# Norm factors by one-column sums, a GpSimd power and identity matmuls, and a forget gate's logarithm by a series, in an eight-core decoder layer

## The reference

```
def rmsnorm(x, g):
    y = xf * lax.rsqrt(jnp.mean(xf * xf, axis=-1, keepdims=True) + EPS)
    return y * g
def layernorm(x, g, b):
    mu = mean(x); var = mean((x - mu) ** 2)
    return (x - mu) * lax.rsqrt(var + EPS) * g + b

h = rmsnorm(x, g_mix_pre)
a_val, a_gate, q, k, v, f_logit = split(h @ w_in)
u = causal_depthwise_conv(a_val * sigmoid(a_gate), conv_w, conv_b)    # width 31
conv_out = silu(layernorm(u, conv_ln_g, conv_ln_b))
log_f = log_sigmoid(f_logit + b_forget)                               # 8 heads
c = cumsum(log_f)                                                     # over tokens
attn = softmax(q k^T / 8 + c[t] - c[s], causal) v                     # 8 heads of 64
x = x + rmsnorm(concat(conv_out, attn) @ w_out, g_mix_post)
h = rmsnorm(x, g_ffn_pre)
x = x + rmsnorm((silu(h @ w_gate) * (h @ w_up)) @ w_down, g_ffn_post) # 2816 wide
```

## Time and profile before

| | |
|---|---|
| median of 3 runs | 2541.02 us (2537.87 to 2663.91) |
| profiled execution, slowest of 8 cores (core 1) | 2540.7 us |
| all cores | 2524.0 to 2540.7 us |
| TensorE busy | 2392.3 us (94%) |
| ScalarE busy | 1604.2 us (63%) |
| VectorE busy | 994.6 us (39%) |
| GpSimd busy | 531.4 us (21%) |
| granted TensorE clock, mean of core 1 | 0.976 |

### The profile page before, as it was taken

How to read it: one execution, slowest core, us unless ns; L and a number is a source line. 1 busy time by engine, 2 the same in 40 slices (tenths; PEclk the granted TensorE clock), 3 DMA queues, 4 the chain that set the end, 5 groups by cost and what they waited for, 6 DMA issues and landing times.

```text
span 2540.7 us, 53568 instructions; the slowest of 8 cores (2524.0 to 2540.7 us)
## 1 busy us (share of the span) xinstructions
PE 2392.3 (94%) x19688; PEld 1214.4 (48%) x19688; DVE 994.6 (39%) x1505; ACT 1604.2 (63%) x1951; POOL 531.4 (21%) x870
## 2 busy tenths in 40 slices
PE   6898999999999889999999999999999999999895
PEld 2353444545454444554554555555555555554342
DVE  3435343443434443243244233424324332443643
ACT  2166667777775666776677677767767767773311
POOL 0141312212121420240131013013013101302301
PEclk9899999999999999999999999999999999999998
DMA  6873856757566766675535535544553563454543
GB/s 145 202 168 105 196 133 161 167 124 181 129 145 162 159 156 150 157 179 161 178 111 170 175 118 150 177 149 125 181 172 107 158 190 107 151 153 137 163 144 95
DMA packets 206893, 386.85 MB, mean 152 GB/s; under 512 B 27776, under 2 KB 109952, under 8 KB 206512
## 3 DMA queue, kind: packets, MB, share of 16 engines
q1 hardware_dynamic: 173408, 299.08, 40.9%
q0 software_dynamic: 33232, 84.34, 15.5%
HBM read 356.22 MB, written 69.11 MB: 167 GB/s over the span
## 4 chain that ended last, share of the span: by engine, by line
PE 80%; ACT 8%; DVE 4%; issue 3%; DMA 2%; POOL 1%; SPq 0%; DVEq 0%; ACTq 0%; POOLq 0%
PE pbig L369 80%; ACT s_pt L1054 3%; DMA s_xs<-xT 1%; ACT s_sq L475 1%; DVE s_tmp L845 1%; ACT L381 1%; DMA s_wout<-w_out 1%; POOL s_pt L1059 1%; DVE s_hT L462 1%; ACT s_rstd L381 1%; DVE s_x L847 1%; ACT L575 0%; ACT L716 0%; ACT s_m L587 0%; ACT s_rstd L383 0%
## 5 line engine op out<-in xcount | busy, mean ns | idle before, releaser
L1054 ACT ACTIVATE s_pt<-pbig 128x1024 bf16<-128x1024 f32 x1088 | 1101.9, 1021 | 497.1 <-PE pbig L369 490.0
L369 PE MATMUL pbig<-s_h,s_wr 128*128 128x512 bf16 x2816 | 710.7, 382 | 8.4 <-DVE s_sa L893 8.3
L369 PE MATMUL pbig<-s_qr,s_kr 68*128 68x512 bf16 (+2 forms) x2304 | 672.4, 374 | 37.4 <-ACT s_pt L1054 34.2
L369 PEld LDWEIGHTS pbig<-s_vr,s_pt 128*128 128x128 bf16 x8832 | 418.9, 98 | 281.7 <-issue 46.8
L369 PE MATMUL pbig<-s_vr,s_pt 128*128 128x65 bf16 x8832 | 460.1, 194 | 11.1 <-POOL s_pt L1059 8.1
L369 PEld LDWEIGHTS pbig<-s_h,s_wr 128*128 128x128 bf16 x2816 | 260.8, 98 | 296.9 <-issue 22.1
L893 DVE SCALAR_TENSOR_TENSOR s_sa<-s_th,pbig 128x512 f32<-128x512 f32 x176 | 120.9, 687 | 518.3 <-ACT s_th L892 495.7
L369 PEld LDWEIGHTS pbig<-s_qr,s_kr 68*128 68x128 bf16 x2304 | 186.6, 99 | 184.7 <-issue 68.2
L369 PE MATMUL pbig<-s_actA,s_wr 128*128 128x512 bf16 x1024 | 264.1, 380 | 0.9 <-DVE s_mix L926 0.9
L406 POOL TENSOR_TENSOR s_ssA<-s_ssA,s_sqr 128x512 f32<-128x512 f32 x112 | 153.0, 1366 | 507.3 <-ACT s_sqr L399 505.5
L1059 POOL TENSOR_SCALAR_AFFINE_SELECT s_pt<-s_pt 128x128 bf16<-128x128 bf16 x256 | 85.4, 339 | 807.7 <-ACT s_pt L1054 778.9
(11 more groups left out here) (129 smaller groups left out, 1899.1 us busy)
## 6 DMA issues: line engine op xcount, KB each, us to landing
s_kr<-k_s SPq DMA_DIRECT2D x288, 160.0 KB, 4.2
s_wr<-wg_b SPq DMA_DIRECT2D x88, 512.0 KB, 4.1
s_wr<-wu_b SPq DMA_DIRECT2D x88, 512.0 KB, 4.4
s_wr<-wd_b SPq DMA_DIRECT2D x128, 352.0 KB, 3.2
s_vr<-v_s SPq DMA_DIRECT2D x288, 130.0 KB, 3.9
s_xs<-xT POOLq DMA_DIRECT2D x48, 512.0 KB, 5.9
s_u<-u_s POOLq DMA_DIRECT2D x32, 540.0 KB, 10.7
s_x<-xT POOLq DMA_DIRECT2D x32, 512.0 KB, 5.4
```

Of the source, the lines that this page charges most:

```text
L369: P.op("pe", lambda e: e.matmul(out, lhsT=lhsT, rhs=rhs, start=start, stop=stop, **kw), reads=reads, writes=[wkey])
L1054: P.op("act", lambda e: e.activation(out=p[:], in_=pbig[:, 2 * s:2 * s + 2, :], func=AF.Exp), reads=[PB(2 * s), PB(2 * s + 1)], writes=p.keys)
```

## The change

- `norm_tail` goes. `norm_rows` takes its place for all RMS norms. The squares become the weights and a single column of ones moves through: for each block of 128 tokens one column of sums, tokens on partitions (`row_sums`: 4 blocks x 8, or x 2, one-column matmuls; token blocks are the outer loop). VectorE scales and adds eps on a 128x4 tile, GpSimd raises it to the power -0.5, and splits the result into bf16 high and low parts (`hilo`). A deferred `spread` turns it back: for each block of 128 tokens two matmuls, weights the high or low column broadcast to 128 columns with stride zero, moving operand the identity, 128 columns; then one ScalarE copy of 512 columns into `rstd`.
- The spread is put ahead of the steps that were deferred, as their first item. First tick 3 instead of 2 (and with `every` 2 the first product at tick 5); `sq_steps` of `A2` starts at 6 or 7 instead of 4, the stores of `N2` at 9 instead of 7. In the last `N2` and behind a flush it follows at once.
- `conv_ln`: sums as columns in one bank instead of two; mean, variance on VectorE on 128x4 tiles, power on GpSimd, two spreads (mean and factor, 16 matmuls, two copies). The 512-column variance operations go.
- `c_chain`: Exp of minus the absolute value on ScalarE; the logarithm of 1 + t becomes a series in t/(t+2) with its steps in VectorE operations on 128x64 tiles, deferred over four ticks; the deferred list starts one tick earlier and is five items longer.
- The load of `identb` moves from after the first norm to the start, on GpSimd's DMA queue ahead of the V weights. A constant tile of -0.5 takes the place of eps.

The diff, cut to its core:

```diff
-    def norm_tail(b, r, scale, ncol=CH):
-
-        P.op("act", lambda e: e.activation(out=r[:, 0:ncol], in_=pb[b][:, 0:ncol], func=AF.Ln, bias=epsb[:, 0:1], scale=scale),
-             reads=[PB(b)] + epsb.keys, writes=r.keys)
-        P.op("act", lambda e: e.activation(out=r[:, 0:ncol], in_=r[:, 0:ncol], func=AF.Exp, scale=-0.5), reads=r.keys, writes=r.keys)
+    def row_sums(t, ks, b, c0, nb=4):
+
+        for tb in range(nb):
+            yield from group(len(ks), lambda n: t[:, ks[n], tb * 128:(tb + 1) * 128], lambda n: ones_bf[:, 0:1], pb[b][:, c0 + tb:c0 + tb + 1],
+                             lambda n: ones_bf.keys + [t.keys[ks[n]]], b, cost=0.03, step=8)
+
+    def spread(n, c0, nb, r, fn=None):
+
+        R, C = nhl[n], r
+        b = bank()
+        for tb in range(nb):
+            for h in range(2):
+                mm(pb[b][:, tb * 128:(tb + 1) * 128], R[:, h, c0 + tb:c0 + tb + 1].to_broadcast([128, 128]), identb[:], h == 0, h == 1,
+                   R.keys + identb.keys, PB(b))
+        P.op("act", lambda e: e.activation(out=C[:, 0:128 * nb], in_=pb[b][:, 0:128 * nb], func=AF.Copy), reads=[PB(b)], writes=C.keys)
+
+    def hilo(n, lo, hi):
+        R, H = nrr[n], nhl[n]
+        P.op("pool", lambda e: e.tensor_copy(out=H[:, 0, lo:hi], in_=R[:, lo:hi]), reads=R.keys, writes=H.keys)
+        P.op("pool", lambda e: e.tensor_tensor(out=H[:, 1, lo:hi], in0=R[:, lo:hi], in1=H[:, 0, lo:hi], op=ALU.subtract),
+             reads=R.keys + H.keys, writes=H.keys)
+
+    def norm_rows(t, ks, scale, r, nb=4):
+
+        n = nrot.next()
+        S_, R = nst[n], nrr[n]
+        b = bank()
+        yield from row_sums(t, ks, b, 0, nb)
+        P.op("dve", lambda e: e.tensor_scalar(out=S_[:, 0:nb], in0=pb[b][:, 0:nb], scalar1=scale, scalar2=EPS, op0=ALU.mult, op1=ALU.add),
+             reads=[PB(b)], writes=S_.keys)
+        P.op("pool", lambda e: e.tensor_tensor(out=R[:, 0:nb], in0=S_[:, 0:nb], in1=mhalf[:, 0:nb], op=ALU.pow),
+             reads=S_.keys + mhalf.keys, writes=R.keys)
+        hilo(n, 0, nb)
+        return lambda: spread(n, 0, nb, r)
...
-        yield from stats(sq, 8, b)
-        norm_tail(b, rstd, 1.0 / D)
-        defer("h", [scale_by(xs, V_GPRE, rstd, hT[i % 3], k) for k in range(8)], 2, every)
+        bc = yield from norm_rows(sq, range(8), 1.0 / D, rstd)
+        defer("h", [bc] + [scale_by(xs, V_GPRE, rstd, hT[i % 3], k) for k in range(8)], 3, every)
...
-        P.op("act", lambda e: e.activation(out=et[:], in_=zt[:], func=AF.Exp, scale=-1.0), reads=zt.keys, writes=et.keys)
-        P.op("act", lambda e: e.activation(out=lt[:], in_=et[:], func=AF.Ln, bias=1.0, scale=1.0), reads=et.keys, writes=lt.keys)
+        P.op("dve", lambda e: e.scalar_tensor_tensor(out=et[:], in0=zt[:], scalar=-1.0, in1=zt[:], op0=ALU.mult, op1=ALU.max),
+             reads=zt.keys, writes=et.keys)
+        P.op("act", lambda e: e.activation(out=et[:], in_=et[:], func=AF.Exp, scale=-1.0), reads=et.keys, writes=et.keys)
+
+        def log1():
...
-        defer("c", [part2, nop] + [part2a(tb) for tb in range(8)] + [part2b, part2c, nop, nop, part3, nop, nop, part4], 3)
+        defer("c", [log1, log2(13, 7), log2(7, 1), log3, nop, part2, nop] + [part2a(tb) for tb in range(8)] + [part2b, part2c, nop, nop, part3, nop, nop, part4], 2)
...
-        yield from stats(sq, 4, b1)
-        b2 = bank()
-        yield from stats(sq, 4, b2, 4)
...
-        P.op("act", lambda e: e.activation(out=lrs[:], in_=m2[:], func=AF.Ln, bias=epsb[:, 0:1], scale=1.0), reads=m2.keys + epsb.keys, writes=lrs.keys)
-        P.op("act", lambda e: e.activation(out=lrs[:], in_=lrs[:], func=AF.Exp, scale=-0.5), reads=lrs.keys, writes=lrs.keys)
+        yield from row_sums(sq, range(4), b1, 0)
+        yield from row_sums(sq, range(4, 8), b1, 4)
...
+        P.op("pool", lambda e: e.tensor_tensor(out=R[:, 4:8], in0=S_[:, 4:8], in1=mhalf[:, 0:4], op=ALU.pow),
+             reads=S_.keys + mhalf.keys, writes=R.keys)
+        hilo(n, 0, 8)
...
-        defer("x1", [resid(mix, V_GPOST, X, ob) for ob in range(8)], 2, 1 if j == 0 else 2)
-        defer("x1", sq_steps(X, 8, ssA, hlA), 4, 1 if j == 0 else 2)
+        bc = yield from norm_rows(hlA, range(2), 1.0 / D, rstd)
+        defer("x1", [bc] + [resid(mix, V_GPOST, X, ob) for ob in range(8)], 3, 1 if j == 0 else 2)
+        defer("x1", sq_steps(X, 8, ssA, hlA), 6 if j == 0 else 7, 1 if j == 0 else 2)
```

More of the change, by code:

```diff
@@ L931, in N2 @@
         flush("sqy")
-        b = bank()
-        yield from stats(hlA, 2, b)
-        norm_tail(b, rstd, 1.0 / D)
+        bc = yield from norm_rows(hlA, range(2), 1.0 / D, rstd)
         def out(g):
@@ L938, in N2 @@
         if j == NOWN - 1:
+            bc()
             for n, ob in enumerate((0, 6, 1, 2, 7, 3, 4, 5)):
```

66 lines of the change are left out of this document (41 added, 25 removed).

## The result

| | before | after |
|---|---|---|
| median | 2541.02 us | 2614.53 us (2612.26 to 2614.90 without the one long execution) |
| ratio of the two, 95% interval | | 1.0289 [1.0269, 1.0309]: slower |
| profiled execution, slowest core | 2540.7 us | 2610.7 us |
| TensorE busy, slowest core | 2392.3 us | 2402.8 us |
| ScalarE busy | 1604.2 us | 1482.0 us |

What follows compares the result with a forecast made beforehand. TensorE, busy 2392.3 of 2540.7 us, was taken as the bound. Pauses -36, clock -11, TensorE's work -2 and the longer chain +29 gave -20 us, so 2521 us, range 2485 to 2560.

Steps and rivals of the forecast that it cites:

- The hinge, table loads: ScalarE: only the logarithm forces table reloads; without it one load is expected and 92.4 us of loads go.
- the hidden part: TensorE's pauses behind table loads: 5.9 us more that the listing hides, added to 41.7 us of listed pauses.
- TensorE's work: Matmuls removed and added in the norms nearly cancel, -2 us; stride-zero identity weights were taken to cost nothing.
- The power: GpSimd's power -0.5 in each norm, taken as 0.5 us, within 0.2 to 1.4.
- the slow rival: GpSimd's power takes microseconds and spreads stall; the gain is gone at 3.3 us, 2629 us at 5; chance 0.08.
- The sum of the pauses: TensorE's waits: 36 us of relief from ScalarE against +29 us for the longer chain, 3 of them clock.
- -36 of relief: TensorE's pauses behind ScalarE's table loads: three quarters of 47.6 us come back, bounds 0 and 48.
- new chain: Norms' longer path through VectorE, GpSimd, identity matmuls and copy: +29 us including 3 of clock, bounds +9 and +60.
- The clock: Projection stage, 130 to 1000 us: 11 us of lost clock come back with fewer pauses, bounds 0 and 35.
- The exposed chain at the start: First four norms, flushed at once: the new chain costs 1.3 us more each, +5 us.
- The order of the sums: Summing block by block makes the very first norm do three quarters of its sums after the last square, +1 us.
- The deferred spreads: The chain fits within three ticks for most spreads; queues for the other 38 cost 0.15 us each, +6 us.

Runs made afterwards that it cites:

- e9: The changed kernel unedited, run once more; its one timed execution took 2604.39 us, 1.0245 of before.
- e6: The changed kernel with the first four pre-norms as before, squares as outer loop of the sums, and 64 columns of ones instead of one; 1.0049 of before.
- e3: The changed kernel with the pre-norms of chunks 0 to 3 as before (wide sums, Ln and Exp on ScalarE); 1.0133 of before.
- e15: The changed kernel with the yields of e4 but sums still in the order of the token blocks; 1.0233 of before.
- e4: The changed kernel with the row-sum loops exchanged (squares outside, token blocks inside) and a yield after every second square; 1.0142 of before.
- e14: The kernel before with only the logarithm's series added, its VectorE steps issued at once behind the exponential, deferred list as before; 1.0146 of before.
- e10: e11 with row sums also in the pre-norms of chunks 7 to 15; 0.9924 of before.
- e11: The changed kernel with all pre-norms and late norms as before, leaving convolution, halo and series, with 64-column sums and squares outside; 0.9994 of before.

## Why the prediction was wrong

- **The hinge, table loads.** Right. One load is left of 73, ScalarE's busy time is 1481 us on core 1 (forecast: near 1475), and the pauses for `s_pt` are 11.7 us (forecast: under 15). The pauses for causal selects are 3.6 us, from 8.1. So 34.2 + 8.1 - 11.7 - 3.6 = 27 us of listed pause came back; with the hidden part that I added, the 36 us were a little high, by under 10.
- **TensorE's work.** Right. In the timeline of after,

```profile
452.11 0.54 PE L373 MATMUL pbig<-s_ones_bf,s_sq 128*128 128x1 bf16 x16
```

  sixteen one-column matmuls are listed with 0.54 us where nothing holds them up, (0.54 - 0.16)/15 = 0.025 us each (forecast: 0.026), and eight identity matmuls with 0.61 us, (0.61 - 0.16)/8 = 0.056 (forecast: 0.057). The stride of zero shows no cost. Listed work counted at full clock falls by 6 to 8 us as a mean (forecast: 2).
- **The power.** 1.07 us, where I took 0.5 within 0.2 to 1.4: inside the bounds, and far from the 3.3 us that the slow rival needed. That rival's mechanism, a spread that stands behind its power, did happen, with a power of a third of the length: 31.8 us of pauses, which I had put at 10 to 20.
- **The sum of the pauses.** This step failed. By my terms (-36 of relief, +26 of new chain without its 3 us of clock) pauses should have shrunk by 10 us; as a mean they grew by 34 (e9: 40). The relief was nearly right, so the sum missed on the side of the chain: on core 1 the pauses for squares are 25 us more, those for `nhl` 32. The two terms are taken up below.
- **The clock.** This step failed too, by sign and by size. I gave back 11 us and charged 3 for new pauses; measured are 43 us more on core 1, and 40 or more as a mean, of which 26 to 42 fall where TensorE has work. The step read the low spans as a consequence of pauses for ScalarE, and concluded that fewer such pauses would shorten them. It didn't ask what TensorE does in and around the new waits: eight short matmuls between two pauses, and one-column sums paced by squares. Behind the second norm the clock is at 0.50 for 10.2 us, through the spread and the projection, where it was for 6.8. e6 shows that at an unchanged order wider sums alone return 13 us of the clock's part. Of the 68 us by which the mean span grew, 56 are in this term, but 13 of the 56 fall in pauses and are counted there too.
- **The exposed chain at the start.** +5 for four norms, by a sum of 3.8 us for one. From the last sum to the first product it is 5.06, 5.05, 8.44 and 5.09 us on core 1, against 2.58, 2.51, 2.51 and 2.50 before, so +13.5 in all. The p of 0.5 was half of the 1.01 us listed there, the handovers were short, and the eight matmuls take 1.01 us instead of 0.6 at the low clock. In the third the series stood in front of the norm on VectorE, a meeting of two parts that no term of mine had. e3's 40 us contain, beyond this, the clock and what follows downstream.
- **The order of the sums.** Priced at +1, for the first norm. This failed: I saw that the first norm can do three quarters of its sums only after its last square, and not that the other fifteen pre-norms are summed while ScalarE still makes squares. The wait for squares doubled (25.0 to 49.6 us on core 1; outside the first norm 7.2 to 31.6), and e15 against e4 puts 23 us on the order. The very first norm, the one that I charged, lost nothing: its first product starts at 24.99 us, at 25.02 before.
- **The deferred spreads.** 38 of them at 0.15 us. The chain of 1.1 + 1.07 us does fit in three ticks, and most spreads have no pause. But `nhl` has 18 pauses on core 1, not the handful of flushed ones: 12.8 us in chunks 0 to 3, 19.0 us in the 14 others, where I had put 15 us on all late spreads and flushes together. GpSimd stood 216 us in front of its powers, and with it the loads and selects behind them; what that cost them no run shows.
- **The series.** Priced at nothing. It costs 9 us alone and 37 in one burst. The cover that I named, VectorE's 60% idle time, is a mean over the run; at the end of `p_kv` it isn't there, as e14 and the norm of chunk 2 show.
- **Chances.** The failure isn't in one rival that was given too little. Slower by over 2% stood only on a slow power; no case had several waits that each lower the clock. Even my bounds taken together at their worst, nothing gained and +60 for the chain, give 2541 - 2 + 60 = 2599 us, short of 2614: the clock's bound was 0, and beyond the 3 us charged under the chain a loss was not among its values. And the range, at 2560, stopped well before that.

## What to carry to other kernels

A pause of TensorE can have a second price, the granted clock behind it: split each span into span x (1 - clock) and the rest before trusting a sum of waits, count of the first only what falls where TensorE has work, and let the clock's term have both signs. When sums change from wide matmuls to columns, look at which operand becomes stationary, for it sets the order in which inputs are needed, and put the new form only where no flush stands behind it and other work fills TensorE (here chunks 7 to 15, 0.7% gained by e10 against e11, and 1.6% lost in chunks 0 to 3 by e3). Look also at what else the change puts into the same engine's list at that place. And before a part is priced by the table loads that it removes, count whose neighbour shares them.
